# Prompt attention of a hybrid decoder trunk: where ScalarE takes the tanh of a gate projection

## The reference

```
h = h + 0.5 * swiglu(rmsnorm(h), ffn1);  x = rmsnorm(h);  z = x @ w_in + b_in
branches = [conv, retention, GLA, differential attention](z)
gate = sigmoid(gates of z);  merged = sum over branches of (branch @ w_branch) * gate
h = h + merged @ w_out;  h = h + 0.5 * swiglu(rmsnorm(h), ffn2)
```

## Time and profile before

| | |
|---|---|
| median of 3 runs | 3239.86 us (3236.12 to 3242.86) |
| the profiled execution, its own time | 3235.98 us |
| span from its first to its last instruction | 3234.4 us |
| PE busy | 3092.7 us, 96% of the span |
| PEld busy | 2949.1 us, 91% |
| DVE busy | 1527.4 us, 47% |
| ACT busy | 928.7 us, 29% |
| mean granted TensorE clock | 0.977 of full speed |
| attention over the prompt | 688.70 to 816.12 us in layer 0, 2289.45 to 2416.96 us in layer 1 |

### The profile page before, as it was taken

One profiled execution on the slowest core, in us unless ns is written; L12 is line 12 of the kernel. 1 busy time (PEld: TensorE's weight loads), 2 busy tenths in 40 slices (PEclk: granted clock), 3 DMA queues, 4 the chain that ended last, 5 costly groups with the idle time before them and its releaser, 6 DMA issues.

```text
span 3234.4 us, 56531 instructions
## 1 busy us (share of the span) xinstructions
PE 3092.7 (96%) x22332; PEld 2949.1 (91%) x22332; DVE 1527.4 (47%) x2355; ACT 928.7 (29%) x1351; POOL 121.0 (4%) x219
## 2 busy tenths in 40 slices
PE   7999989999899999999999999899898999999998
PEld 6999989877778999999999999888777789999998
DVE  4444232565556654443344442326555466544433
ACT  3222223334214232222222222233342152322222
POOL 0000001210000000000000000012100000000000
PEclk9999999999889999999999999999998899999999
DMA  4222215541213322222222222336312133222222
GB/s 151 79 78 82 88 58 175 177 160 60 77 63 134 136 75 82 78 84 85 85 79 84 78 82 88 109 126 193 132 60 88 60 141 123 80 83 79 78 87 93
DMA packets 102092, 319.32 MB, mean 99 GB/s; under 512 B 13503, under 2 KB 30063, under 8 KB 100272
## 3 DMA queue, kind: packets, MB, share of 16 engines
q1 hardware_dynamic: 89424, 275.82, 25.5%
q0 software_dynamic: 12512, 41.43, 4.1%
HBM read 290.02 MB, written 28.51 MB: 98 GB/s over the span
## 4 chain that ended last, share of the span: by engine, by line
PE 87%; issue 4%; DVE 3%; ACT 3%; POOLq 1%; DMA 1%; POOL 1%; ACTq 0%; DVEq 0%
PE ps L907 77%; PE ps L1023 2%; PE ps L1008 1%; PE ps L919 1%; PE ps L1232 1%; ACT hT L708 1%; PE ps L1113 1%; PE ps L1076 1%; POOLq L466 1%; PE ps L1099 0%; ACT p_prob L720 0%; PE ps L1114 0%; DMA rets_out<-ss 0%; POOL vpage L467 0%; PE ps L1134 0%
## 5 line engine op out<-in xcount | busy, mean ns | idle before, releaser
L907 PE MATMUL ps<-x_hi,w_hi 128*128 128x296 f32 x4416 | 998.8, 308 | 38.9 <-ACT hT L708 28.8
L907 PE MATMUL ps<-x_lo,w_hi 128*128 128x296 f32 x4416 | 973.0, 302 | 0.0
L907 PE MATMUL ps<-x_hi,w_lo 128*128 128x296 f32 x4416 | 972.2, 302 | 0.0
L1338 DVE TENSOR_TENSOR w_lo<-w_raw,w_hi 128x1024 fp32r<-128x1024 f32 x416 | 509.0, 1225 | 724.6 <-ACT w_hi L577 624.3
L907 PEld LDWEIGHTS ps<-x_hi,w_hi 128*128 128x128 f32 x4416 | 726.6, 192 | 68.9 <-issue 54.5
L907 PEld LDWEIGHTS ps<-x_hi,w_lo 128*128 128x128 f32 x4416 | 731.5, 192 | 0.0
L907 PEld LDWEIGHTS ps<-x_lo,w_hi 128*128 128x128 f32 x4416 | 727.9, 192 | 0.0
L577 ACT ACTIVATE w_hi<-w_raw 128x1024 fp32r<-128x1024 f32 x328 | 346.0, 1057 | 1122.2 <-DVE gu L1386 443.3
L907 PE MATMUL ps<-hid_hi,w_hi 128*128 128x296 f32 x1408 | 307.5, 300 | 0.0
L907 PE MATMUL ps<-hid_lo,w_hi 128*128 128x296 f32 x1408 | 305.3, 298 | 0.0
L907 PE MATMUL ps<-hid_hi,w_lo 128*128 128x296 f32 x1408 | 304.9, 298 | 0.0
(11 more groups left out here) (297 smaller groups left out, 2886.5 us busy)
## 6 DMA issues: line engine op xcount, KB each, us to landing
w_raw<-wstream SPq DMA_DIRECT2D x420, 512.0 KB, 3.3
kpage<-cache_k SPq DMA_DIRECT2D x128, 128.0 KB, 3.0
vpage<-cache_v POOLq DMA_DIRECT2D x128, 128.0 KB, 3.2
gate_rows<-hT SPq DMA_DIRECT2D x48, 296.0 KB, 2.1
d_sg<-gate_rows SPq DMA_DIRECT2D x16, 888.0 KB, 4.6
hT<-h_in SPq DMA_DIRECT2D x4, 592.0 KB, 8.3
h_rows<-hT SPq DMA_DIRECT2D x2, 1184.0 KB, 5.5
hT<-h_rows SPq DMA_DIRECT2D x2, 1184.0 KB, 9.2
```

What stands on the lines that cost most here:

```text
L907: mm = pe.matmul(ps[:, 2 * p + half, 0:HALF], wp[:, k, :], xp[:, k0 + k - blocks[0], half * HALF:(half + 1) * HALF], start=start and k == ...
L1338: v.tensor_tensor(w_lo[:, slot, :, :], w_raw[:, slot, :, :], w_hi[:, slot, :, :].bitcast(F32), ALU.subtract).then_inc(weights_low, 1)
```

## The change

In the odd steps of attention over the prompt, ScalarE takes the tanh of the gate unit first, before it waits for the transposed probabilities and copies them. The high part of the next weight stays at the end of the step. `gate_out` becomes a function of two parts, so that its other callers do as before.

```diff
-            def gate_out(l, f):
+            def gate_activated(l, f):
 
                 quad, slot = l * QUADS + (U_GATES + f) // RING, f % RING
                 act.wait_ge(h_spilled, 16)
@@
                 c = f // EARLY + 8 * (f % EARLY)
                 act.activation(split_cols(hT[:, f % STAGES, :]), pair(3), ACT.Tanh, scale=0.5, bias=hb[:, c:c + 1]).then_inc(gate_tanh, 1)
-                split_high(quad + 1, slot)
+
+            def gate_out(l, f):
+
+                gate_activated(l, f)
+                split_high(l * QUADS + (U_GATES + f) // RING + 1, f % RING)
 
@@
                 for x, (j, h) in enumerate(steps):
                     n = META if j == 0 else P
+                    if x % 2:
+                        gate_activated(l, x // 2)
                     act.wait_ge(prompt_turned, x + 1)
@@
                     if x:
                         placed(x - 1)
                     if x % 2:
-                        gate_out(l, x // 2)
+                        split_high(l * QUADS + (U_GATES + x // 2) // RING + 1, x // 2 % RING)
                 placed(len(steps) - 1)
```

## The result

| | before | after |
|---|---|---|
| median | 3240.82 us (3236.12 to 3242.86, 4 runs) | 3206.91 us (3205.57 to 3214.71, 4 runs) |
| ratio after to before | | 0.9902, 95% interval 0.9883 to 0.9922 |
| span of the profiled execution | 3234.4 us | 3206.0 us |
| attention over the prompt, layer 0 | 127.42 us | 112.67 us |
| attention over the prompt, layer 1 | 127.51 us | 112.68 us |

The change makes the kernel 1.0% faster. The two spans differ by 28.4 us, and the two stages by 14.75 + 14.83 = 29.6 us. So the whole of it comes from attention over the prompt; the rest of the span is 1.2 us longer. "The stage" is attention over the prompt in one layer, and "after" is the changed kernel.

The account below looks back on a forecast made before the run. TensorE's matmuls bound the kernel, so only its idle time or clock matters. Stalls 20.4 us plus clock 8.9 us make 29.3 us; from the 3239.86 us median that gives 3210.6, stated as 3210, range 3202 to 3222.

Parts of the forecast that it names:

- The stalls: Attention over the prompt: TensorE's waits for the tanh, 10.8 us a layer, shrink by 10.2 us, 20.4 for both layers.
- G + 0.93: G is the end of the gate unit; with the tanh first, the next unit could begin 0.93 us later.
- The clock: Half gate units behind stalls in steps 8, 10, 12 regain full clock: 4.4 us a layer, 8.9 for both.
- The first rival: Stalls go, but the clock falls as often, in other steps or the mixers behind: 3219 us, chance 0.23.
- The rule that was cited: Trainium skill's rule: the clock falls only behind idle gaps longer than these stalls, so it would give nothing back.
- The cover of the copies: Step 17: time between VectorE's difference and the next transposes, 2.55 us, of which 1.7 us is left after the change.
- so the cover is no smaller: Steps before 17: exps and difference work on fewer keys while the half unit stays as long, so cover is not less.
- The second and third: Half the gain returns as transposes' waits for VectorE, 3225 us, chance 0.08; or idle time only moves, 3243 us, 0.04.
- The fourth: Idle time joins the transposes and the clock falls behind all nine stalls a layer: 3261 us, slower, chance 0.03.
- The other queues: SyncE's store wait, the weight's high part and GpSimd's retention table cost nothing; the table stays hidden with 8 us to spare.
- The base: Starting time for the sum: the median of the runs, 3239.86 us, 3.9 us above the profiled execution's 3235.98.

Follow-up runs that it names:

- the second pair: The kernel before and the changed kernel each run once more, unedited: 3238.91 and 3209.80 us.
- the late and the middle steps: Changed kernel with the old order back in steps 13, 15, 17 alone (3218.38 us), or in steps 7, 9, 11 alone (3222.53 us).
- the 18 pauses amid full matmuls: Changed kernel with TensorE waiting for one unneeded ScalarE copy in the middle of each even step's half unit but the first: 3234.59 us.
- One more us of delay: Changed kernel with one unneeded ScalarE copy between the tanh and the copies of each odd step: 3210.06 us.
- four copies: Changed kernel with four unneeded ScalarE copies between the tanh and the copies of each odd step: 3323.88 us.

## Why the prediction was right

The forecast was 3210 us in a range of 3202 to 3222; measured were 3206.91. Its sum was 29.3 us; the spans of the profiles differ by 28.4, and those of the second pair by 29.1.

- **The stalls, 10.2 us a layer.** Right: of 10.8 us 0.44 are left behind step 1, and behind step 3 only the 0.14 us of passing the semaphore. TensorE's idle time in the stage fell by 11.16 - 0.94 = 10.2 us. The next unit after step 1 was to begin at G + 0.93; it began at 700.22, with its last matmul ended at 699.29. This was exact, and the kernel with the tanh between copies and exps confirms the same arithmetic on four other stalls.
- **The clock, 4.4 us a layer.** The stage shrank by 14.75 us and not by the 10.35 of the stalls, and the profile's busy time of TensorE by 4.5. That falls need the stall was a guess from three cases. It now stands on 48 stalls of the old order (two profiles of before, the late and the middle steps): 16 have a slow half unit behind them, one in three. In 12 stages without a stall over 0.8 us, and behind the 18 pauses amid full matmuls, there is none but the first half unit. But one in three is a mean over unlike steps. In the four layers of before 11 of the 12 slow half units stand behind steps 7, 9 and 11 (of 12 stalls there) and one behind the other six steps (of 24 stalls), while the old order in the late steps alone gave 2 in 6. Why these steps, no run here shows. So that 4.4 us came out also rests on the fact that three falls a layer are what before usually has: all four of its layers have three.
- **The first rival**, that the falls only move, is refuted. In the stage none is left, and behind it nothing is lost that would pay for it: the rest of the span took 2982.1 us in the repeat of before and 2981.9 in that of after. What it got right is that which stalls are hit can change: step 1 in one execution of before, step 13 in the kernel with the late stalls.
- **The rule that was cited.** By the table "Why this matters for your kernels" of the Trainium skill's page "TensorE: Matmul & The Clock Gate" the clock should not fall behind gaps this short, which fits the pauses. It doesn't fit the stalls of 1.0 to 1.5 us that stand beside transposes and scores. For this case the measurement decides.
- **The cover of the copies, 1.7 us.** Right in step 18, where it is 1.66 us. Wrong was "so the cover is no smaller" for the steps before: it is 1.24 us in step 4. There it had been 3.15 us, but the stall taken out was 1.27 of 1.41 us and not 0.86, and the difference ends 0.6 us later behind the unit, since the copy in step 3 is some 0.5 us late. That enough was left there was in part luck, as the prediction had not worked it out. One more us of delay showed that it holds, with 0.29 us to spare.
- **The other rivals.** The second and third needed the cover gone. The fourth was brought about by force with four copies. Waits at the transposes do pull the clock down, and by more than that rival had it: it counted nine falls of 1.5 us, 13.4 us a layer, and with waits about twice as long the clock alone cost 22 to 30.
- **The other queues** showed nothing: no wait for a store of `gate_rows`, and retention's first product waits 0.37 us for the last copy to `od`, as before.
- **The base.** The prediction counted from the median shown to it, 3239.86. The rest of the distance, 3 us, is within the 7 to 9 us over which runs of one kernel spread, so that 3206.91 and not 3210 was measured says nothing for or against a term. The 1.2 us outside the stage are no more than chance either: the rest of the span took 3234.4 - 254.9 = 2979.5 us in before, 3206.0 - 225.4 = 2980.6 in after, and between 3230.6 - 250.7 = 2979.9 (the pauses) and 3212.8 - 228.1 = 2984.7 (the tanh between) in experiments that leave it alone.

## What to carry to other kernels

An engine with slack can still stall the bottleneck by the order of its own queue: look at what the bottleneck waits for, and whether the instruction that answers stands behind work that nobody is waiting for yet. Before moving it, measure how late the displaced work becomes, and what lies between it and its reader; here a delay of 0.5 us left 1.2 us of cover. Count the clock too: of the 14.75 us a layer, 4.4 were not idle time but matmuls at half speed behind it.

## What was not expected of the hardware

Behind an idle time of 0.9 to 1.5 us in TensorE the granted clock went to 0.50 in 16 of 48 cases when short matmuls (transposes, 128 x 64 products, scores with 32 rows) stood before it, and in 0 of 18 when full matmuls stood on both sides of 1.15 us. 13 of the 16 lie behind steps 7, 9 and 11. Once waits of 2.7 us came in every other step, the mean granted clock of the stage was 0.80 to 0.85, and the slow clock cost 22 and 30 us a layer beside 28 us of waits. A pause amid full matmuls costs 1.41 us for 1.15 us of idle time.
